# Second block laid out anew: two attentions run between layer products, and the first gate layer between small layers

## The reference, cut to what matters

```python
h = rmsnorm_2(x, norm_in_g)
proj = h @ w_in        # 1024 -> q_sb, k_sb, v_sb, gate_sb (512 each), c_q 384, c_kv 256,
                       #         k_rope 32, gate_mla 512, gate_logits 2 x 1024
# stick-breaking attention, 8 heads of 64, queries in blocks of 128, keys s < t
z = q_sb k_sb^T / 8
w = exp(log_sigmoid(z) + sum_{s<j<t} log_sigmoid(-z_j))
y_sb = (w v_sb * silu(gate_sb)) @ w_o_sb
# latent attention (mla), 8 heads, 96-wide queries and keys (64 plain, 32 rotated)
q = rmsnorm_2(c_q) @ w_q_up;  k, v = rmsnorm_2(c_kv) @ w_kv_up
p = softmax(q k^T / sqrt(96)), by chunks of 64 keys
y_mla = (p v_mla * silu(gate_mla)) @ w_o_mla
g = sigmoid(gate_logits + b_gate)
x = x + (g0 * y_sb + g1 * y_mla) @ w_out
return rmsnorm_2(x, norm_f_g)
```

## Time and profile before

| | us |
|---|---|
| median of 3 runs (1944.69 to 1951.93) | 1947.55 |
| the profiled execution, its own time | 1942.64 |
| its span, first to last instruction | 1941.0 |
| PE busy | 1704.8 (88%) |
| DVE busy | 1113.3 (57%) |
| ACT busy | 698.1 (36%) |

### The profile page before, as it was taken

How to read it: one execution, slowest core, us unless ns; L and a number is a source line. 1 busy time by engine, 2 the same in 40 slices (tenths; PEclk the granted TensorE clock), 3 DMA queues, 4 the chain that set the end, 5 groups by cost and what they waited for, 6 DMA issues and landing times.

```text
span 1941.0 us, 23362 instructions
## 1 busy us (share of the span) xinstructions
PE 1704.8 (88%) x8748; PEld 1366.5 (70%) x8748; DVE 1113.3 (57%) x1683; ACT 698.1 (36%) x1073; POOL 47.2 (2%) x88
## 2 busy tenths in 40 slices
PE   2586598999999988999989999999897587899996
PEld 2465476788888767777667888888685376678885
DVE  7979867666556664545446453455634726733343
ACT  2240142333233333444434332333425724633231
POOL 0000011000000000000000000000000000000000
PEclk9998699899999989999998999999897788999998
DMA  7123166243543334333111322322321001122231
GB/s 305 54 69 115 55 222 227 98 151 114 178 163 132 122 137 152 117 134 131 57 66 65 108 70 103 109 88 80 114 68 41 1 25 55 41 76 76 98 120 44
DMA packets 54412, 202.84 MB, mean 105 GB/s; under 512 B 8272, under 2 KB 16848, under 8 KB 41760
## 3 DMA queue, kind: packets, MB, share of 16 engines
q1 hardware_dynamic: 42624, 159.20, 24.3%
q0 software_dynamic: 11712, 42.60, 6.4%
HBM read 194.80 MB, written 6.32 MB: 104 GB/s over the span
## 4 chain that ended last, share of the span: by engine, by line
PE 70%; DVE 16%; issue 5%; ACT 5%; DMA 4%; SPq 0%; DVEq 0%; POOLq 0%; ACTq 0%
PE ps L430 21%; PE ps L431 20%; PE ps L432 20%; DMA adaw<-in_ada_w 3%; DVE w_lo L1145 2%; ACT w_hi L770 2%; PE ps L583 1%; DVE pw L1352 1%; DVE t L1544 1%; DVE ada L1168 1%; PE ps L518 1%; PE ps L527 1%; PE ps L540 1%; PE ps L594 1%; PE ps L607 1%
## 5 line engine op out<-in xcount | busy, mean ns | idle before, releaser
L430 PE MATMUL ps<-xn_hi,w_lo 128*128 128x512 f32 x1264 | 505.2, 400 | 19.1 <-DVE xn_lo L1265 9.9
L431 PE MATMUL ps<-xn_lo,w_hi 128*128 128x512 f32 x1264 | 498.2, 394 | 0.0
L432 PE MATMUL ps<-xn_hi,w_hi 128*128 128x512 f32 x1264 | 498.0, 394 | 0.0
L1145 DVE TENSOR_TENSOR w_lo<-raw,w_hi 128x2048 fp32r<-128x2048 f32 (+3 forms) x145 | 311.7, 2150 | 269.8 <-ACT w_hi L770 269.5
L770 ACT ACTIVATE w_hi<-raw 128x2048 fp32r<-128x2048 f32 (+3 forms) x145 | 260.0, 1793 | 115.2 <-PE ps L432 113.7
L430 PEld LDWEIGHTS ps<-xn_hi,w_lo 128*128 128x128 f32 x1264 | 241.5, 191 | 75.7 <-issue 17.5
L432 PEld LDWEIGHTS ps<-xn_hi,w_hi 128*128 128x128 f32 x1264 | 240.9, 191 | 51.5
L431 PEld LDWEIGHTS ps<-xn_lo,w_hi 128*128 128x128 f32 x1264 | 241.8, 191 | 48.6
L430 PE MATMUL ps<-act_hi,w_lo 128*128 128x512 f32 x352 | 139.1, 395 | 1.1 <-DVE w_lo L1145 1.1
L432 PE MATMUL ps<-act_hi,w_hi 128*128 128x512 f32 x352 | 138.8, 394 | 0.0
L431 PE MATMUL ps<-act_lo,w_hi 128*128 128x512 f32 x352 | 138.8, 394 | 0.0
(11 more groups left out here) (345 smaller groups left out, 2459.4 us busy)
## 6 DMA issues: line engine op xcount, KB each, us to landing
raw<-in_weights SPq DMA_DIRECT2D x97, 1024.0 KB, 4.9
adaw<-in_ada_w POOLq DMA_DIRECT2D x80, 512.0 KB, 4.7
raw<-in_weights SPq DMA_DIRECT2D x16, 768.0 KB, 4.3
raw<-in_weights SPq DMA_DIRECT2D x16, 640.0 KB, 3.8
ada<-in_ada_w SPq DMA_DIRECT2D x8, 1024.0 KB, 16.0
fbias<-f_dram SPq DMA_DIRECT2D x16, 256.0 KB, 3.7
raw<-in_weights SPq DMA_DIRECT2D x8, 512.0 KB, 3.5
h<-in_xT SPq DMA_DIRECT2D x1, 2048.0 KB, 12.2
```

The costliest lines, as they stand in the source:

```text
L430: pe.matmul(bank, lo_w, hi_x, start=start, stop=False)
L431: pe.matmul(bank, hi_w, lo_x, start=False, stop=False)
L432: return pe.matmul(bank, hi_w, hi_x, start=False, stop=stop)
L1145: V.tensor_tensor(w_lo[:, b, 0:words], raw[:, b, 0:words], f32(w_hi[:, b, 0:words]), ALU.subtract).then_inc(split_lo, 1)
```

## The change

It leaves the arithmetic as it is and changes the order, the places in memory and the beats.

1. `LAYERS`: sb_q, sb_k, sb_v and gate_sb are cut into two groups of one chunk each. The order becomes sb_q0, sb_k0, sb_v0, gate_sb0, sb_q1, sb_k1, sb_v1, gate_sb1, mla_c (3), gate_mla (2), g0_0, mla_q0 (2), g0_1, mla_q1 (2), g0_2, mla_k (2), g0_3, mla_v (2), osb_0 to osb_3, then g1_m and omla_m for m = 0 to 3, mix_out.
2. PE: `fox_beats` becomes `beats_of`, used for all three attentions. Stick-breaking takes 12 beats per 32 groups, from gate_sb0 to the first chunk of gate_mla. Mla takes one beat and two beats in turn, one call after each group of osb_0 to osb_3, the rest in g1_0. Both have one pair of score banks (4, 5), one bank for turned weights (6) and one for outputs (7).
3. The norm of c_q is cut in two (`norm_sums`, `norm_spread`), with the halves of g0_0 behind them.
4. The gates are copied out unchanged (`sg_sb`, `sg_mla`), Silu is applied later in SBUF, and the first gate's Sigmoid results are kept (`mgs_of`) and multiplied as osb comes out.
5. First model: ada columns 70 to 75 move into the loop of down01; five are left (76 to 80) where eleven were. In fox_out ACT splits the next chunk before the squares of this one, and up10's first splits follow at once.

```diff
-LAYERS += [("sb_q", 8, 256, 2), ("sb_k", 8, 256, 2), ("sb_v", 8, 256, 2), ("mla_c", 8, 256, 3),
-           ("mla_q", 3, 256, 4), ("mla_k", 2, 256, 2), ("mla_v", 2, 256, 2),
-           ("gate_sb", 8, 256, 2), ("gate_mla", 8, 256, 2)]
+for _g in range(2):
+    LAYERS += [(f"sb_q{_g}", 8, 256, 1), (f"sb_k{_g}", 8, 256, 1), (f"sb_v{_g}", 8, 256, 1), (f"gate_sb{_g}", 8, 256, 1)]
+LAYERS += [("mla_c", 8, 256, 3), ("gate_mla", 8, 256, 2),
+           ("g0_0", 8, 256, 1), ("mla_q0", 3, 256, 2), ("g0_1", 8, 256, 1), ("mla_q1", 3, 256, 2),
+           ("g0_2", 8, 256, 1), ("mla_k", 2, 256, 2), ("g0_3", 8, 256, 1), ("mla_v", 2, 256, 2)]
+LAYERS += [(f"osb_{_m}", 4, 256, 1) for _m in range(4)]
```

PE, the beats of an attention; scores wait until both units before are out of the two banks, a turn waits for the copy of the turn before:

```diff
+            for n in range(4 * pairs + 2):
+                if n < 4 * pairs:
+                    scores(n)
+                if n >= 2:
+                    weigh(n - 2)
                 yield
-                if 1 <= n <= pairs:
+                if 1 <= n <= 4 * pairs:
                     turn(2 * n - 2)
                 yield
-                if 1 <= n <= pairs:
+                if 1 <= n <= 4 * pairs:
                     turn(2 * n - 1)
                 yield
```

PE, where they are taken:

```diff
+        between = spread(beats, (0, 1, 3, 4, 6, 9, 11, 14, 17, 20, 24, 28), 32)
+        layer("gate_sb0", xn_hi, xn_lo, between=between)
...
+        layer("mla_c", xn_hi, xn_lo, between=between)
...
+        norm_sums("cq")
+        layer_part("g0_0", 0, xn_hi, xn_lo, part=(0, 4))
+        norm_spread("cq")
+        layer_part("g0_0", 0, xn_hi, xn_lo, part=(4, 8))
+        layer("mla_q0", cq_hi, cq_lo, (xl, XTILE["cq"]))
+        layer("g0_1", xn_hi, xn_lo)
...
+        def between():
+            for _ in range(1 + steps[0] % 2):
+                next(beats, None)
+            steps[0] += 1
         for m in range(4):
+            layer(f"osb_{m}", osb_hi, osb_lo, (gm_lo, GATED["gate_sb"]) if m == 0 else None, between=between)
```

ACT, stick-breaking, then from the norm of c_q on:

```diff
+        for p in range(4):
+            sb_period(4 * p, later=(lambda: evacuate_beside(2 * p - 1)) if p else None)
+            split_next(first + 2 * p)
+            sb_period(4 * p + 1)
+            sb_period(4 * p + 2)
+            split_next(first + 2 * p + 1)
+            sb_period(4 * p + 3, later=lambda: evacuate_beside(2 * p))
...
+        norm("cq", cq_hi, QL)
+        rounded("ckv", ck_hi)
+        out_of("gate_mla", copy_out(sg_mla), 1)
+        out_of("g0_0", gate_out(0, 0, lambda r: mgs_of[r]))
+        layer("mla_q0", query_out(0))
+        for gate in (sg_sb, sg_mla):
+            for m in range(4):
+                A(gate[:, m], gate[:, m], ACT.Silu).then_inc(sg_ready, 1)
```

First model, DVE:

```diff
-                ada(24 * 2 + 22, 2)
-                dve.wait_ge(mod_copy, 30)
+                dve.wait_ge(mod_copy, 36)
...
-                    layer(name, lambda j, b, i: ada(72 + 3 * n, 3), early=n == 0)
+                    layer(name, lambda j, b, i: ada((76, 77, 79)[n], (1, 2, 2)[n]), early=n == 0)
...
                 with dve.Fori(0, DT // 2 - 1) as i:
                     down(i)
+                    if l == 0 and hf == 1:
+                        for b in range(2):
+                            ada_loop(i * 2 + 70, b)
```

First model, ACT, fox_out:

```diff
-                layer("fox_out", residual("ffn1"), early=True)
-            split_next(FIRST[f"up{l}0"])
+                for i in range(4):
+                    n = FIRST["fox_out"] + i
+                    split_next(n + 1)
+                    residual("ffn1")(n // 2, n % 2, i)
```

More of the change, by code:

```diff
@@ L734, in _ @@
         norm_stat("in2")
[L735 to L744 removed]
+        layer("sb_q0", xn_hi, xn_lo, (xl, XTILE["in2"]))
@@ L929, in attention @@
[L929 to L942 removed]
+            if later:
+                later()
@@ new lines, in gated_hi, with mla_period @@
+        def gated_hi(name, pair, dst, src):
+            act.wait_ge(gm_prod, GATED[name] + pair + 1)
+            A(dst, src[:, pair], ACT.Copy).then_inc(gm_hi, 1)
+        def mla_period(n, later=None):
+            base, pairs = UNIT["mla"], 2 * H2
+            if n < pairs:
+                w = (n % 4 + 1) * P
+                for u in (2 * n, 2 * n + 1):
+                    st = stat[:, u % 4]
+                    act.wait_ge(nm_done, u + 1)
+                    act.wait_ge(tr_done, base + u - 3)
+                    A(pw[:, u % 4, 0:w], ps[:, 4 + u % 2, 0:w], ACT.Exp, bias=st[:, 1:2], scale=QK ** -0.5, accum_out=st[:, 2:3]).then_inc(s_free, 1)
+            if 1 <= n <= pairs:
+                turned_copy(base + 2 * n - 2)
+            if later:
+                later()
+            if 1 <= n <= pairs:
+                turned_copy(base + 2 * n - 1)
+            if n >= 5 and n % 4 == 1:
+                pair = n // 4 - 1
+                gated_hi("gate_mla", pair, omla[pair // 2][:, pair % 2, 0], sg_mla)
@@ new lines, in _ @@
+        layer("mla_q0", query_rope(0))
+        for m in range(4):
+            dve.wait_ge(sg_ready, m + 1)
+            TT(sg_sb[:, m], o_sb[:, m], sg_sb[:, m], ALU.mult).then_inc(gm_prod, 1)
+        for m in range(4):
+            dve.wait_ge(gm_hi, GATED["gate_sb"] + m + 1)
+            TT(osb_lo[:, m], sg_sb[:, m], f32(osb_hi[:, m]), ALU.subtract).then_inc(gm_lo, 1)
+        layer("g0_1")
+        layer("mla_q1", query_rope(4))
+        layer("g0_2")
+        after_layer(dve, "mla_q1")
+        dve.wait_ge(kr_ready, 1)
@@ new lines, in _, with branch_out @@
+        for hd in range(H2 - 1):
+            V.tensor_copy(key_tile(hd)[64:QK], key_tile(H2 - 1)[64:QK]).then_inc(mk_rope, 1)
+        layer("mla_k")
+        layer("g0_3")
+        layer("mla_v")
+        def branch_out(name, m, tiles):
+            n = FIRST[f"{name}_{m}"]
+            j, b = n // 2, n % 2
+            for r in range(2):
+                dve.wait_ge(done[b], done_value(j, r))
+                TT(tiles(r), ps[:, 2 * b + r], tiles(r), ALU.mult).then_inc(evac[b], 1)
+        after_layer(dve, "g0_3")
@@ new lines, in _ @@
+        dve.wait_ge(sg_ready, 8)
+        for n in range(18):
+            following = FIRST["osb_0"] + n // 4
+            mla_period(n, later=(lambda: split_next(following)) if n % 4 == 1 else None)
+            if n and n % 4 == 0:
+                m = n // 4 - 1
+                branch_out("osb", m, lambda r: mgs_of[2 * m + r])
+        for m in range(4):
+            if m:
+                layer(f"g1_{m}")
+            layer(f"omla_{m}")
+            after_layer(dve, f"g1_{m}")
+            branch_out("omla", m, lambda r: hn[:, r])
```

554 lines of the change are left out of this document (277 added, 277 removed).

## The result

The changed kernel takes **1889.51 us** (median of four runs, 1888.07 to 1891.86) against 1946.65 for the kernel before beside it: ratio 0.9704, 95% interval 0.9685 to 0.9722. The forecast was 1896, with a range from 1875 to 1921. The profiled execution took 1888.30 us, with a span of 1886.6. Against the profiled execution of the kernel before (span 1941.0) that is 54.4 us less, where the sum of the steps said 51.6. The sum of the steps accounts for 2.7 of the 6.4 us by which the forecast was too high. One of the six executions of the kernel of experiment 8 took 3507.46 us at a recorded granted clock of 1.000, its cause is open, and the ratio given there leaves it out.

What follows compares the result with a forecast made beforehand. PE, busy 88% of the span, was taken as the bound, with gains only where it idles or runs at half clock. 47.2 + 5.5 - 4.8 + 3.7 = 51.6 off 1942.6 gives 1891.0, plus 4.9: 1896; range 1875 to 1921.

Steps and rivals of the forecast that it cites:

- the sum of the steps: Whole kernel: gains of 47.2, 5.5 and 3.7 less a loss of 4.8, 51.6 us off the profiled execution.
- The largest term: Stick-breaking and mla_c, second block: attention run between PE's products gains 47.2 us, bounds 41 and 50.
- Stick-breaking: Second block: attention costs PE 10.7 us per pair; its chain of 28.0 fits the pair's room of 32.5.
- The rival's chain of 35.3: Stick-breaking: all splits and evacuations lie on the chain, 35.3 us per pair against 32.5; time 1910, chance 0.24.
- The rival without overlap: Attention beats always late, products start only then; 22 us more per stick-breaking pair, time 1985, chance 0.05.
- Small layers: Second block, mla_q0 to osb_0 seams: 56.0 us become 50.5, including 14.8 of stalls; gain 5.5, bounds 0 and 9.
- four of these are long enough to bring the half clock back for some 0.9 us each: Small layers: four of the late seams each add some 0.9 us of half clock, 3.5 in all.
- Mla: Mla attention run with osb: 72.4 us become 77.2, 18.1 per pair; loss 4.8, bounds -10 and +6.
- Gates: Stored gates add eight Silus of some 0.6 us on ACT, hidden while g0_1's 10.9 us on PE cover them.
- the row: Profile row for ACT table loads: one takes 1.28 us, used instead of the skill page's 2.7 per switch.
- First model: Moved ada columns and fox_out order: norm +2.3, fox start +5.0, down01 -2.4, fox_out -1.2; gain 3.7, bounds -1 and 8.
- The start of fox: First model, fox layer: with six fewer ada columns, 5.0 of 6.6 us come back; one tile wait may return.

Runs made afterwards that it cites:

- experiment 8: Changed kernel with mla_q and g0 chunks alternating, mla's beats over 48 groups, turned-unit copy between the Exps, fox_out's old order; 1867.8 us, repeated 1867.03.
- experiment 6: Changed kernel with each mla_q chunk followed by a full g0 chunk, and ACT's splits ahead of evacuations; 1879.57 us.
- Experiment 5: Changed kernel with gate_mla's second chunk copied out before c_q's norm, and g0_3's weights split before mla_k's key copies; 1883.38 us.
- experiment 7: Two kernels, each the changed one with one part put back: ada columns, 1898.63 us; fox_out's old order, 1888.66 us.

## Why the prediction was right

From its first product to the last norm's sums the second block is 50.0 us shorter (520.4 before, 470.4 after); the prediction had named 40 to 55 as the test of the whole. The largest term and the reasons for it held; two smaller terms were right in sum only.

*Stick-breaking: right, by the reason given.* Forecast 42.8 us for the attention between products, measured 43.2; forecast 142 us from gate_sb0 to gate_mla's first chunk, measured 152.2 less 10.9 = 141.3 from the first beat on. PE waited 2.6 us in four pairs for the subtraction, under 1 us a pair as said. The chain of 28.0 per pair is 26.6 in the changed kernel, so the reserve of 4.5 us per pair was there (5.9 and 5.5 in the second and third pair). The rival's chain of 35.3 lies 8.7 us above it. The rival without overlap had no part in it.

*Small layers: right in sum, by errors that cancel.* The stalls were put at 14.8 us and are 10.3: 1.9, 2.6, 2.7 and 3.1 where I had 2.9, 3.1, 3.5 and 3.9, and none at mla_q1 and osb_0. The half clock behind them was put at 3.5 and is about 6: PE's 82.7 us less 43.6 of g0, 27.7 of small layers and 3.4 of norm (4.5 in the forecast) leave 8.0, and the same sum leaves 2.0 in experiment 6, for five full chunks at a clock of 1.00. The step that failed is "four of these are long enough to bring the half clock back for some 0.9 us each". Experiment 5 shows the same size from the other side: 2.5 us less of waits shortened the stretch by 5.6.

*Mla: right.* 18.1 us per pair forecast, 18.5 measured in the second and third pair, and the loss 5.5 instead of 4.8. 4.5 of it is idle time: 10.7 us where the kernel before idled 6.2 in the same stages. The other 1.0 is PE's busy time, 178.8 against 177.8 for the same products and attention.

*Gates: right.* No wait of PE leads to a Silu. Of the table loads on the path one shows: 1.28 us before the first Exp, with 0.8 us of waiting at the second scores.

```profile
1679.91 1.28 ACT L1204 ACT_TABLE_LOAD   x1
...
1682.06 1.13 PE L536 MATMUL ps<-m_k,m_q 96*128 96x256 f32 x4 [0.79 <-ACT pw L969]
```

All four loads of the new order (at 1604, 1614, 1626 and 1680 us) took 1.28 us. The Trainium skill, page "ScalarE: Activation LUTs", section "Rules for kernel authors", budgets about 2.7 us for a switch, by which the time would have been 1899 (the estimate in the prediction); the measurement decides for the row.

*First model: right in sum, with two terms mis-sized against each other.* Before the norm 2.3 us were gained, as forecast (wait 6.1, now 3.8). The start of fox gave 7.7 instead of 5.0: both waits went entirely, no tile wait came back, and 1.1 us went beyond the 6.6 that I could name. down01 cost 1.6 instead of 2.4, two further waits of 0.6. fox_out cost 2.4 instead of 1.2, which giving back the old order removes in full in the profile of experiment 8 and by half in that of experiment 7; 0.75 was lost behind it, up to the second block, and 0.5 had been lost ahead of down01.

## What to carry to other kernels

Between two chains that alternate on one engine ask for both numbers: the length of the chain per unit and the work that stands between its beats. As long as the second is larger, it is the spreading that matters (41 us here with the same work, 26 of them waits and the rest half clock). When small products need much post-processing, put a large product behind each small one instead of behind each pair: a stall is the post-processing of one chunk plus the next split, less the one chunk that runs meanwhile. And a stall of 2 to 3 us can cost about twice its length, as the clock falls behind it (in experiment 5: 2.5 us of waits, 5.6 us of time).

## What was not expected of the hardware

A stall's price varies between executions of one kernel. Twenty microseconds from the end of the same wait of 2.89 us on, in the changed kernel's first profile and in its repeated run:

```profile
1747.24:1767.24 20.00, 18.17 (x107) 13.33 (x108) 6.75 (x14) 6.87 (x12) 0.00 (x0) 1.00 0.15 48
```

```profile
1746.85:1766.85 20.00, 18.15 (x99) 12.49 (x100) 6.79 (x14) 6.87 (x12) 0.00 (x0) 0.91 0.15 50
```

With the same waits the clock was 1.00 in one and 0.91 in the other, and 107 matmuls were done where the other did 99. The stretch from the first mla scores to the last norm took 189.5 and 191.3 us. Differences under 2 us between single profiles of such kernels are no evidence.

A product that follows an attention step takes longer to start: on PE's timeline of the changed kernel 0.33 us lie between the starts of the first two matmuls, 0.23 between the next ones.

```profile
1562.61 0.50 PE L445 MATMUL ps<-xn_hi,w_lo 128*128 128x512 f32 x1
1562.94 0.39 PE L446 MATMUL ps<-xn_lo,w_hi 128*128 128x512 f32 x1
1563.17 0.40 PE L447 MATMUL ps<-xn_hi,w_hi 128*128 128x512 f32 x1
```

0.10 us in some 36 places would be 3.6 us in mla (an estimate), but PE's busy time there is only 1.0 us above that of the kernel before; where the rest went was not tested. Not tried either: mla alone with four score banks, as in the kernel before, beside the new layout of the small layers, which by the balance above could give back the 5.5 us lost there; and a cut of the attention into fewer, longer beats.
